# Half 0 of the merged rows turned by VectorE and two DMA queues, with the last gate item moved

## The reference

```
h = RMSNorm(x)
pool | diff q, k, v | stick q, k, v | fox q, k, v | forget logits | gate logits = h @ w_in
y_n = branch_n(...) @ w_branch[rows of branch n]          # n = 0..3: pool, diff, sticks, fox
merged = sum_n sigmoid(gate_logit_n + b_gate_n) * y_n     # each 256 x 1024
x = x + merged @ w_out
x = x + SwiGLU(RMSNorm(x))
```

## Time and profile before

| | |
|---|---|
| median of 3 runs | 849.12 us (849.07 to 849.25) |
| the profiled execution | 849.36 us, its span 847.6 us |
| TensorE | 842.3 us, 99% of the span |
| VectorE | 605.3 us, 71% |
| ScalarE | 445.5 us, 53% |
| GpSimd | 114.9 us, 14% |
| DMA | 170.43 MB, mean 201 GB/s |

### The profile page before, as it was taken

One profiled execution on the slowest core, in us unless ns is written; L12 is line 12 of the kernel. 1 busy time (PEld: TensorE's weight loads), 2 busy tenths in 40 slices (PEclk: granted clock), 3 DMA queues, 4 the chain that ended last, 5 costly groups with the idle time before them and its releaser, 6 DMA issues.

```text
span 847.6 us, 11122 instructions
## 1 busy us (share of the span) xinstructions
PE 842.3 (99%) x4126; PEld 699.2 (83%) x4126; DVE 605.3 (71%) x890; ACT 445.5 (53%) x650; POOL 114.9 (14%) x89
## 2 busy tenths in 40 slices
PE   9999999999999999999999999999999999999998
PEld 7888888888888888888888888888888888888887
DVE  7885977679677666665479668868687776666643
ACT  6657645754454455444365675557543644444431
POOL 0750201004502000000005402010054000000000
PEclk9999999999999999999999999999999999999999
DMA  9846666477567777666566365764965577666651
GB/s 340 286 164 179 200 214 192 148 243 232 184 199 244 203 220 218 202 218 217 173 185 191 109 191 172 237 202 123 296 189 169 177 236 205 205 202 220 222 188 50
DMA packets 100934, 170.43 MB, mean 201 GB/s; under 512 B 12944, under 2 KB 26768, under 8 KB 100880
## 3 DMA queue, kind: packets, MB, share of 16 engines
q1 hardware_dynamic: 100448, 169.07, 63.8%
q10 hardware_dynamic: 432, 0.66, 0.3%
HBM read 160.77 MB, written 3.15 MB: 193 GB/s over the span
## 4 chain that ended last, share of the span: by engine, by line
PE 99%; DMA 1%; ACT 0%; issue 0%; DVE 0%; ACTq 0%
PE bulk L1761 30%; PE bulk L1765 30%; PE bulk L1762 30%; PE bankAB L1526 2%; DMA raw<-in_w_in_dram 1%; PE bankT L1673 0%; PE bulk L1808 0%; PE bankAB L1662 0%; PE bulk L1789 0%; PE bankAB L1620 0%; PE bulk L1795 0%; PE bankAB L1535 0%; PE bankO L1631 0%; PE bankO L1683 0%; PE bankO L1691 0%; PE bankO L1685 0%
## 5 line engine op out<-in xcount | busy, mean ns | idle before, releaser
L1087 DVE TENSOR_TENSOR w_lo<-raw,w_hi 128x1024 fp32r<-128x1024 f32 (+1 forms) x288 | 360.2, 1268 | 116.9 <-ACT w_hi L812 114.4
L812 ACT ACTIVATE w_hi<-raw 128x1024 fp32r<-128x1024 f32 (+1 forms) x286 | 295.5, 1047 | 206.7 <-PE bulk L1765 202.6
L1761 PE MATMUL bulk<-w_hi,hT_hi 128*128 128x512 f32 (+1 forms) x880 | 342.8, 390 | 0.0
L1762 PE MATMUL bulk<-w_lo,hT_hi 128*128 128x512 f32 (+1 forms) x880 | 339.3, 386 | 0.0
L1765 PE MATMUL bulk<-w_hi,hT_lo 128*128 128x512 f32 (+1 forms) x880 | 336.3, 386 | 0.0
L1761 PEld LDWEIGHTS bulk<-w_hi,hT_hi 128*128 128x128 f32 x880 | 165.3, 188 | 33.1 <-issue 0.5
L1765 PEld LDWEIGHTS bulk<-w_hi,hT_lo 128*128 128x128 f32 x880 | 165.0, 188 | 33.3
L1762 PEld LDWEIGHTS bulk<-w_lo,hT_hi 128*128 128x128 f32 x880 | 165.4, 188 | 32.0
L1761 PE MATMUL bulk<-w_hi,aT_hi 128*128 128x512 f32 x174 | 67.8, 390 | 0.0
L1765 PE MATMUL bulk<-w_hi,aT_lo 128*128 128x512 f32 x174 | 67.7, 389 | 0.0
L1762 PE MATMUL bulk<-w_lo,aT_hi 128*128 128x512 f32 x174 | 67.7, 389 | 0.0
(11 more groups left out here) (239 smaller groups left out, 715.6 us busy)
## 6 DMA issues: line engine op xcount, KB each, us to landing
raw<-in_w_in_dram SPq DMA_DIRECT2D x110, 512.0 KB, 4.5
raw<-in_w_ffn_up_dram SPq DMA_DIRECT2D x80, 512.0 KB, 4.1
raw<-in_w_ffn_down_dram SPq DMA_DIRECT2D x44, 512.0 KB, 3.6
raw<-in_w_branch_dram SPq DMA_DIRECT2D x20, 512.0 KB, 5.3
raw<-in_w_out_dram SPq DMA_DIRECT2D x16, 512.0 KB, 3.3
wide<-wide SPq DMA_DIRECT2D x160, 32.0 KB, 2.7
bias<-in_b_gate_dram SPq DMA_DIRECT2D x16, 256.0 KB, 4.9
raw<-in_w_ffn_up_dram SPq DMA_DIRECT2D x16, 256.0 KB, 3.4
```

The costliest lines, as they stand in the source:

```text
L812: act.activation(w_hi[:, g % RING, :, 0:width], raw[:, g % RAW, :, 0:width], ACT.Copy).then_inc(hi_ready, 1)
L1087: vec.tensor_tensor(w_lo[:, g % RING, :, 0:width], raw[:, g % RAW, :, 0:width], w_hi[:, g % RING, :, 0:width].bitcast(F32), ALU.subtract). ...
L1761: pe.matmul(dst, hi, whi, start=(k == ks[0]), stop=False)
L1762: pe.matmul(dst, hi, wlo, start=False, stop=False)
```

## The change

- The last gate item (7: the second half of the fox gate) moves behind the first half's branches. Units: gates 0 to 6 at 28 to 55, branches of half 0 at 56 to 60, gate 7 at 61 to 64, branches of half 1 at 65 to 69 as before.
- The sigmoid of branch 3 is done in two halves of 512 columns (`sigmoid_last`), each with its own event.
- `tr_merged` 0 leaves TensorE. VectorE turns the blocks at slot 63 from `wide` into `v_d`. Of the 16 transfers from `v_d` to `o_d` eight are issued by SP at slot 67 and eight by ScalarE at slot 64 (`half_spread`, ahead of its split of unit 68). `merged_evac` 0 reads `o_d`, on ScalarE at slot 68 in place of 69.
- The diff rows are turned at VectorE's slot 48 in place of 49, ahead of the fox softmax; the transfers by DRAM follow one slot earlier.
- The value product of the third diff head (`pv`, "diff", 2) goes from TensorE's slot 39 to 42, its evacuation on VectorE from 39 to 41; `tr_forget` goes from 39 to 37, ahead of the third head's `tr_probs`, and its evacuation on ScalarE from 39 to 37. `gate` 7 on VectorE goes from slot 60 to 65.

```diff
-ITEMS += [(("gate", g), "w_in", [(OFF["gate"] + g * NC, NC)], KD) for g in range(8)]
+GATES = [(("gate", g), "w_in", [(OFF["gate"] + g * NC, NC)], KD) for g in range(8)]
...
-ITEMS += [(("branch", j, n), "w_branch", [(j * NC, NC)], KB[n]) for j in range(2) for n in range(4)]
+ITEMS += GATES[:7] + [(("branch", 0, n), "w_branch", [(0, NC)], KB[n]) for n in range(4)]
+ITEMS += GATES[7:] + [(("branch", 1, n), "w_branch", [(NC, NC)], KB[n]) for n in range(4)]
...
-    (37, "scores", "diff", 3), (37, "pv", "diff", 1), (39, "tr_probs", "diff", 2), (39, "pv", "diff", 2), (39, "tr_forget"), (42, "tr_probs", "diff", 3), (42, "scores", "fox", 0), (42, "pv", "diff", 3),
-    (47, "tr_probs", "fox", 0), (47, "scores", "fox", 1), (47, "pool_a"), (47, "pv", "fox", 0), (50, "pool_b"),
-    (52, "tr_probs", "fox", 1), (56, "pv", "fox", 1), (68, "tr_merged", 0),
-    (73, "tr_merged", 1)]
+    (37, "scores", "diff", 3), (37, "pv", "diff", 1), (37, "tr_forget"), (39, "tr_probs", "diff", 2), (42, "pv", "diff", 2),
+    (42, "tr_probs", "diff", 3), (42, "scores", "fox", 0), (42, "pv", "diff", 3), (47, "tr_probs", "fox", 0),
+    (47, "scores", "fox", 1), (47, "pool_a"), (47, "pv", "fox", 0), (50, "pool_b"), (52, "tr_probs", "fox", 1),
+    (56, "pv", "fox", 1), (73, "tr_merged", 1)]
...
-TURN_AT = {"fox": 33, "diff": 49}
+TURN_AT = {"fox": 33, "diff": 48, "merged": 63}
 SPREAD_AT = {}
 BY_DRAM = ('fox', 'diff')
+SPREAD_AT.setdefault(TURN_AT["merged"] + AHEAD, []).extend([("merged", 0), ("merged", 1)])
...
+    (55, "diff_evac", 0), (56, "pv_evac", "fox", 1), (57, "sigmoid_last", 0, 0), (57, "sigmoid_last", 0, 1),
+    (64, "half_spread", "merged"), (65, "sigmoid_last", 1, 0), (66, "sigmoid_last", 1, 1), (68, "merged_evac", 0),
...
+    (57, "pv_evac", "fox", 1), (63, "turn", "merged"), (65, "gate", 7), (69, "merged_evac", 0), (71, "merged_evac", 1)]
...
+        def spread_group(engine, layer, stage, a):
+
+            turned, spread, blocks = turning(stage)
+            engine.wait_ge(block_turned, nth(block_turned, layer, stage))
+            for b in range(NQUAD):
+                engine.dma_start(spread[b * QUAD:(b + 1) * QUAD, a, :, 0:blocks, :],
+                                 turned[a * QUAD:(a + 1) * QUAD, b, :, 0:blocks, :]).then_inc(block_spread, 16)
...
+            def half_spread(layer, stage):
+                for a in (2, 3):
+                    spread_group(act, layer, stage, a)
...
+            def sigmoid_last(layer, j, t):
+                act.wait_ge(gate_ready, nth(gate_ready, layer, (6 + j, t)))
+                g = wide[:, t, 3 * D + j * NC:3 * D + (j + 1) * NC]
+                act.activation(g, g, ACT.Sigmoid).then_inc(gate_open, 1)
...
+                if j == 0:
+                    wait_spread(act, layer, "merged")
+                    for t in range(TT):
+                        lhs_part(layer, ("merged", 0, t), by_quads(hT[0], (0, 4), t), spread_columns("merged", t, (0, 4)))
+                    return
...
+                    if j == 0:
+                        lhs_rest(layer, ("merged", 0, t), by_quads(hT[1], (0, 4), t), spread_columns("merged", t, (0, 4)),
+                                 by_quads(hT[0], (0, 4), t))
+                        continue
...
+                elif stage == "merged":
+                    turn_blocks(layer, stage, *(merged_ready, (0, 1)), lambda t: merged(t)[:, 0:NC])
```

More of the change, by code:

```diff
@@ L175, in stage_parts @@
     if stage == "tr_merged":
-        return [((stage, args[0], t), ("AB", "TO")[args[0]][t]) for t in range(TT)]
+        return [((stage, args[0], t), "TO"[t]) for t in range(TT)]
     raise ValueError(stage)
@@ L212 @@
     (27, "softmax", "diff", 0), (29, "probs_evac", "diff", 0), (30, "pf"), (30, "fox_forget"), (32, "softmax", "diff", 1),
-    (36, "softmax", "diff", 2), (37, "probs_evac", "diff", 1), (38, "softmax", "diff", 3), (38, "probs_evac", "diff", 2),
-    (39, "forget_evac"), (39, "fox_evac", "fq"), (39, "fox_evac", "fk"), (41, "probs_evac", "diff", 3),
+    (36, "softmax", "diff", 2), (37, "probs_evac", "diff", 1), (37, "forget_evac"), (38, "softmax", "diff", 3),
+    (38, "probs_evac", "diff", 2), (39, "fox_evac", "fq"), (39, "fox_evac", "fk"), (41, "probs_evac", "diff", 3),
     (42, "softmax", "fox", 0), (46, "sigmoid", 0, 0), (46, "probs_evac", "fox", 0), (48, "softmax", "fox", 1),
     (48, "pool_evac_a"), (48, "sigmoid", 0, 1), (48, "sigmoid", 1, 0), (48, "sigmoid", 1, 1), (48, "pv_evac", "fox", 0),
-    (49, "pool_evac_b"), (52, "probs_evac", "fox", 1), (53, "sigmoid", 2, 1), (53, "sigmoid", 2, 0), (55, "diff_evac", 1),
-    (55, "diff_evac", 0), (56, "pv_evac", "fox", 1), (60, "sigmoid", 3, 0), (61, "sigmoid", 3, 1), (69, "merged_evac", 0),
+    (49, "pool_evac_b"), (52, "probs_evac", "fox", 1), (53, "sigmoid", 2, 0), (53, "sigmoid", 2, 1), (55, "diff_evac", 1),
+    (55, "diff_evac", 0), (56, "pv_evac", "fox", 1), (57, "sigmoid_last", 0, 0), (57, "sigmoid_last", 0, 1),
+    (64, "half_spread", "merged"), (65, "sigmoid_last", 1, 0), (66, "sigmoid_last", 1, 1), (68, "merged_evac", 0),
     (72, "merged_evac", 1)]
@@ L227 @@
     (33, "turn", "fox"), (36, "gate", 1), (37, "softmax", "diff", 2), (37, "maxima", "diff", 3), (37, "pv_evac", "diff", 1),
-    (39, "pv_evac", "diff", 2), (39, "softmax", "diff", 3), (39, "fox_evac", "fq"), (39, "fox_evac", "fk"), (40, "gate", 2),
+    (39, "softmax", "diff", 3), (39, "fox_evac", "fq"), (39, "fox_evac", "fk"), (40, "gate", 2), (41, "pv_evac", "diff", 2),
     (41, "maxima", "fox", 0), (41, "softmax", "fox", 0), (42, "pv_evac", "diff", 3), (44, "gate", 3), (47, "maxima", "fox", 1),
-    (48, "diff_norm"), (48, "pv_evac", "fox", 0), (49, "softmax", "fox", 1), (49, "gate", 4), (49, "pool_evac_b"),
-    (49, "turn", "diff"), (52, "gate", 5), (55, "diff_evac", 1), (55, "diff_evac", 0), (56, "gate", 6),
-    (57, "pv_evac", "fox", 1), (60, "gate", 7), (69, "merged_evac", 0), (71, "merged_evac", 1)]
+    (48, "diff_norm"), (48, "pv_evac", "fox", 0), (48, "turn", "diff"), (49, "softmax", "fox", 1), (49, "gate", 4),
+    (49, "pool_evac_b"), (52, "gate", 5), (55, "diff_evac", 1), (55, "diff_evac", 0), (56, "gate", 6),
+    (57, "pv_evac", "fox", 1), (63, "turn", "merged"), (65, "gate", 7), (69, "merged_evac", 0), (71, "merged_evac", 1)]
 def evacuations(mixing, *branches):
@@ L459, in turning @@
             blocks = FF_BLOCKS[stage[1]] if kind == "act" else 4
-            return (*{"act": normed_place, "dq": late, "diff": late}.get(kind, early), blocks)
+            return (*{"act": normed_place, "diff": late, "merged": late}.get(kind, early), blocks)
         def spread_columns(stage, t, blocks):
@@ L547, in build @@
         gate_ready = signal("gate_ready", [(g, t) for g in range(8) for t in range(TT)])
-        gate_open = signal("gate_open", [(n, t) for n in range(4) for t in range(TT)])
+        gate_open = signal("gate_open", [(n, t) for n in range(3) for t in range(TT)] + [(3, j, t) for j in range(2) for t in range(TT)])
         gated = signal("gated", [(j, n, t) for j in range(2) for n in range(4) for t in range(TT)])
@@ L680, in _ @@
                     for stage, a in SPREAD_AT.get(u, ()):
-                        turned, spread, blocks = turning(stage)
                         if a == "out":
                             rows_to_dram(sp, layer, stage)
-                            continue
-                        if a == "back":
+                        elif a == "back":
                             rows_from_dram(sp, layer, stage)
[L687 to L691, removed]
+                        else:
+                            spread_group(sp, layer, stage, a)
                     if layer == 0:
@@ L998, in merged_evac @@
                     lhs_part(layer, ("merged", j, t), hT[0][:, 4 * j:4 * j + 4, t * P:(t + 1) * P],
-                             bank[("AB", "TO")[j][t]].rearrange("p (k q) -> p k q", k=4))
+                             bank["TO"[t]].rearrange("p (k q) -> p k q", k=4))
             def ff_gate(layer, p):
@@ L1029, in _ @@
                           diff_evac=diff_evac, gate=nothing, sigmoid=sigmoid, branch=nothing,
-                          merged_evac=merged_evac, ff_gate=ff_gate, ff_up=nothing, turn=nothing, act_turn=nothing, act_evac=act_evac)
+                          merged_evac=merged_evac, ff_gate=ff_gate, ff_up=nothing, sigmoid_last=sigmoid_last, half_spread=half_spread, turn=nothing, act_turn=nothing, act_evac=act_evac)
             def first_hi(k):
@@ L1385, in branch @@
                     wait_item(vec, layer, ("branch", j, n), t)
-                    vec.wait_ge(gate_open, nth(gate_open, layer, (n, t)))
+                    vec.wait_ge(gate_open, nth(gate_open, layer, (n, t) if n < 3 else (n, j, t)))
                     g = wide[:, t, n * D + j * NC:n * D + (j + 1) * NC]
@@ L1391, in merged_evac @@
                 for t in range(TT):
+                    if j == 0:
+                        lhs_rest(layer, ("merged", 0, t), by_quads(hT[1], (0, 4), t), spread_columns("merged", t, (0, 4)),
```

(6 more changed lines are left out.)

## The result

The changed kernel takes 857.6 us (855.92 to 858.3, 4 runs) against 849.18: a ratio of 1.0096, interval 1.0084 to 1.0108. It is 8.4 us slower than before where 4.7 were forecast, and lies above the range, which ended at 856.5. The profiled execution took 857.61 around a span of 855.8.

The account below looks back on a forecast made before the run. TensorE's own work was taken as the bound, busy 842.3 of 847.6 us. Per layer -0.87 - 0.83 + 2.85 + 1.2 = +2.35 us, twice 4.7, gave a median of 853.8 us; range 849.0 to 856.5.

Parts of the forecast that it names:

- The gains: On TensorE: 0.87 us a layer from eight transposes removed, 0.83 from the third head's value product no longer waiting; 1.70 together.
- The first wait: Unit 66, diff product of half 1, waits for VectorE's gate 7 behind ScalarE's issues: 2.6 us, 2.85 a layer with restart.
- the same zero: Start of VectorE's evacuation of the first half's diff product, from which the terms up to unit 66 were counted.
- The rival of cheap issues at 0.45: Issues on ScalarE cost 0.45 us each or less, so the wait at unit 66 is shorter: 850.1 us; chance 0.13.
- the one in which the whole gain arrives: Issues do not hold back ScalarE's split, so -1.70 us a layer with 0 to 0.9 of wait: 847.0 us; chance 0.15.
- The clock: Rival: TensorE, idle 2.6 us, falls to 1.2 GHz for one unit a layer, adding 2.7 us: 859; chance 0.03.
- The second wait: Unit 70, first output projection item, waits for VectorE's evacuation of the sticks' product of half 1: 1.2 us a layer.
- The port's part: VectorE and GpSimd alternate at their shared port, delaying split and merged_evac: 0.7 us of wait at unit 70.
- The part of the late gate: The late gate 7 puts VectorE another 0.5 us behind, raising the wait at unit 70 from 0.7 to 1.2.
- The rival in which VectorE goes first: VectorE goes ahead of GpSimd at the port, wait at unit 70 only 0.1 to 0.5 us: 851.8; chance 0.20.
- What was hidden: VectorE's block turn (1.29 us), SP's eight issues (4.8 us), the landings and the earlier diff branch cost TensorE nothing.
- The rival of late diff rows: Diff rows return over 1.4 us after 177.5, delaying unit 57: one to 2 us a layer more, 856.8; chance 0.07.

Follow-up runs that it names:

- experiment 1: The kernel before with only the third diff head's value product, its evacuation and the forget transposes moved: 847.39 us, ratio 0.9979.
- experiment 8: As experiment 7, with GpSimd's first pair of additions of half 1 cut from 512 to 8 columns, part of the sum left out: 845.71 us, ratio 0.9959.
- experiment 2: The changed kernel with half 0's merged rows turned by TensorE again at slot 68, without block turn and its transfers: 847.43 us, ratio 0.9979.
- experiment 3: The changed kernel with ScalarE's eight issues one slot later, at 65, behind its split of unit 68: 850.16 us, ratio 1.0016.
- experiment 5: The changed kernel with six of ScalarE's issues at slot 64 and two at slot 65: 853.03 us, ratio 1.0044.
- experiment 6: The changed kernel with VectorE's gate 7 at slot 64, ahead of its split of unit 68, the issues unmoved: 853.76 us, ratio 1.0052.
- experiment 4: The changed kernel with all sixteen issues on SP, none on ScalarE: 853.36 us, ratio 1.0044.
- experiment 7: The changed kernel with ten issues on SP and six on ScalarE, two each at slots 64, 65 and 66: 847.87 us, ratio 0.9985.

## Why the prediction was wrong

**The gains.** Right. The value product was worth 0.83 us a layer; experiment 1 gave 0.9. The eight transposes were worth 0.87: experiment 8, which has no wait left, lies 1.7 us below experiment 1, and its layer 0 (195.93 us against 196.80 between the same transposes) is 0.87 shorter.

**The first wait.** The mechanism was right link by link: GpSimd's additions, turn, issues, split, split, gate (experiments 2, 3, 5 and 6). Its size was a little low, 3.19 us lost at unit 66 against 2.85. My terms up to the gate's first tile add up to 21.5, not to the 21.6 that I wrote; measured from the same zero, 188.90, that tile ends at 21.90 (210.04 + 0.76). Nearly all of the 0.4 between them is the issues: 5.18 us from the first one to the split (207.81 - 202.63) against 4.8, at 0.64 from one to the next instead of 0.6. The rival of cheap issues at 0.45 is wrong, and so is the one in which the whole gain arrives.

**The clock.** This is the step that failed. I set its chance at 0.03 on the ground that the longest wait in the trace of before, 0.6 us, had left the clock alone, and that no wait there was long enough to show more. That row said nothing of a wait over four times as long, one that I had forecast myself. The mechanism was named, and its price, 2.7 a layer, was too high, yet its chance was far too low: it came in both layers and cost 1.6 us in layer 0 and 1.5 in layer 1, products up to 0.43 us apart instead of 0.227. The traces: behind 3.0 us of idleness the granted clock fell to 0.50 in both layers of the changed kernel, behind 2.8 and 2.0 in experiment 4; behind 2.3 it fell once and stayed twice (in experiment 6 it fell in layer 0 and stayed in layer 1, in experiment 3 it stayed), and behind 1.8 and less it stayed at 1.00 (experiments 5 and 7). The length of one wait alone does not decide: of the eleven runs of experiment 3, one kernel, five had a mean clock of 0.998 and six of 1.000. What decides among them stays open. The Trainium skill, "TensorE: Matmul & The Clock Gate", section "What's actually happening", says that an idle TensorE falls to the lower clock, and these traces agree. With 1.6 and 1.5 in the sum, the forecast of 853.8 would have been 856.9. The spread of the runs, 855.92 to 858.3, goes with it: their mean granted clock reads 0.998 for the shortest, 0.996 for the two of 857.6 and 0.994 for the longest. The shortest lies inside my range; that would have been the chance of the clock, not a better forecast.

**The second wait.** The mechanism was right, the size within its bounds: 0.91 us against 1.2 taken. The port's part was right: the low parts took 2.38 us, held as forecast, and experiments 7 and 8 price it at 0.75 us of wait, 0.7 forecast. The part of the late gate was not: VectorE was on time again for the evacuation of unit 67 (218.29, after 0.37 of idleness), for TensorE too was late, by 1.6 us more than I thought, from the clock. That this is the reason is argued, not isolated; experiment 5 speaks for it, where the clock stayed and unit 70 waited 1.1. The rival in which VectorE goes first is wrong.

**What was hidden.** The block turn, SP's eight issues and the earlier diff branch cost nothing, as said; experiment 2 shows it for the diff branch, experiment 8, with both gains whole, for the turn and for ten issues on SP. The rival of late diff rows falls: VectorE ended them at 178.7 where I had 180.4. Sixteen issues on SP were not hidden (experiment 4).

**The sum.** Forecast +2.35 a layer, measured +4.13 in layer 0. The missing 1.8 are 1.6 of clock and 0.3 at unit 66, mostly issues, less 0.3 at unit 70, and 0.2 of products that start slowly behind the two. The range ended at 856.5 because the clock was the case left out; a rival that follows from the forecast itself cannot be left out at 0.03.

## What to carry to other kernels

Moving work off the bound engine pays only if the new work's issues stand nowhere ahead of something that this engine waits for: walk the other engine's queue behind every inserted instruction, transfers included, and spread them so that each gap holds what it can. Where a wait of a few microseconds is forecast for TensorE, put the lower clock behind it into the sum (here some 1.5 us a fall), or give it a chance of its own that is not small. When two engines contend for a port, put the short instruction that something waits for ahead of the long one that has time.

## What the runs showed of the hardware that was not expected

In these runs an issue on ScalarE did not wait for the end of the activation ahead of it. In experiment 3 the split of unit 68 starts at 202.53 with 1.06 us of length, and the first issue starts at 202.58. It is only what stands behind the issues that is held, here until 208.71. So an issue right behind a long activation is partly free. Experiment 7 uses this for its issues at slots 65 and 66; those of slot 65 in its timeline:

```profile
203.76 1.06 ACT L830 ACTIVATE w_hi<-raw 128x1024 fp32r<-128x1024 f32 x1 [3.05 <-issue]
203.79 1.16 ACTq L600 DMA_DIRECT2D o_d<-v_d  x2
```

Single issues now and then take twice as long: 1.31 us on ScalarE in experiment 3 while SP issued too, but also 1.36 on SP in experiment 4, where no other queue issued. These two stand in the chains of layer 0:

```profile
205.14 1.31 ACTq L598
```

```profile
204.74 1.36 SPq L598
```
